# The state scans of a two-layer mixer run three heads ahead of attention instead of one

## The reference

```python
def s5_branch(u, ...):                      # state branch, 512 channels, 2048 complex states
    lam_bar = jnp.exp(lam * dt)
    bu = jnp.einsum('gph,bsgh->bsgp', b_bar, ug)
    _, h = lax.associative_scan(combine, (a, bu), axis=1)       # h[t] = lam_bar*h[t-1] + bu[t]
    y = jnp.real(jnp.einsum('ghp,bsgp->bsgh', c_mat, h)) ...
    y = jax.nn.gelu(y + d * uf)
    return y * jax.nn.sigmoid(y @ glu_w + glu_b)

def hybrid_mixer(x, ...):
    proj = x @ w_in                          # gives z_sgu, z_ssm, q, k, v, gates
    br_a = spatial_gating(jax.nn.gelu(z_sgu), ...)
    br_b = s5_branch(z_ssm, ...)
    br_c = moba_attention(q, k, v)           # 8 heads of 64, here plain causal attention
    g = sigmoid(gates)
    merged = g[0] * (br_a @ w_a) + g[1] * (br_b @ w_b) + g[2] * (br_c @ w_c)
    return merged @ w_out
```

## Time and profile before

| what | value |
|---|---|
| median of 3 runs | 2191.64 us (2191.57 to 2194.16) |
| profiled execution | 2188.97 us, span 2187.2 us |
| busy over the span | PE 94%, DVE 39%, ACT 21%, POOL 11% |
| mean granted TensorE clock | 0.974 of full speed |

### The profile page before, as it was taken

The page is one execution under the profiler, slowest core; times in us unless marked ns, Lnnn a source line. Parts: engine busy times, 40 slices in busy tenths (PEclk is TensorE's granted clock), DMA queues, the critical chain, the costliest instruction groups (busy, mean ns, idle before and its releaser), DMA issues.

```text
span 2187.2 us, 34182 instructions
## 1 busy us (share of the span) xinstructions
PE 2061.2 (94%) x13823; PEld 1387.8 (63%) x13823; DVE 847.5 (39%) x1551; ACT 469.6 (21%) x880; POOL 248.0 (11%) x233
## 2 busy tenths in 40 slices
PE   7988999999998999999889999999997999999996
PEld 5776868864676786886344565699985443444342
DVE  1288230001237822000238865645456333233324
ACT  2255200000325510000032125433333101110110
POOL 2367100000037700000000001100000000000000
PEclk9999999999999999999989999999997899999998
DMA  7422444442642254444452224400012899999993
GB/s 236 149 83 89 179 138 154 154 154 85 199 145 91 83 192 140 150 149 149 153 188 74 92 100 154 155 3 4 3 44 87 336 396 395 395 412 395 392 395 154
DMA packets 138672, 385.45 MB, mean 176 GB/s; under 512 B 16903, under 2 KB 64367, under 8 KB 127409
## 3 DMA queue, kind: packets, MB, share of 16 engines
q1 hardware_dynamic: 138545, 383.61, 47.2%
HBM read 382.54 MB, written 1.05 MB: 175 GB/s over the span
## 4 chain that ended last, share of the span: by engine, by line
PE 41%; DVE 5%; ACT 2%; issue 1%; DMA 1%; DVEq 0%; POOL 0%; ACTq 0%; POOLq 0%
PE psum L1243 9%; PE psum L2820 9%; PE psum L1990 8%; PE psum L2844 5%; PE psum L2755 3%; PE psum L1442 1%; PE psum L2406 1%; ACT arena L1600 1%; PE psum L2059 1%; DVE arena L3033 1%; DVE arena L2955 1%; PE psum L2832 1%; PE psum L2008 1%; DMA ring<-in_w_ada_dram 1%; PE psum L2773 0%
## 5 line engine op out<-in xcount | busy, mean ns | idle before, releaser
L364 PE MATMUL psum<-arena,ring 128*128 128x256 f32 x1728 | 389.4, 385 | 17.2 <-DVE arena L935 15.9
L364 PEld LDWEIGHTS psum<-arena,ring 128*128 128x128 f32 x1728 | 330.3, 192 | 73.5 <-issue 16.6
L573 PE MATMUL psum<-arena,ring 128*128 128x256 f32 (+1 forms) x1536 | 306.8, 361 | 3.2 <-ACT arena L624 3.2
L573 PEld LDWEIGHTS psum<-arena,ring 128*128 128x128 f32 x1536 | 270.5, 189 | 39.3 <-ACT arena L624 4.0
L1990 PE MATMUL psum<-arena 64*64 64x64 f32 (+1 forms) x4320 | 179.9, 237 | 4.6 <-issue 1.9
L624 ACT ACTIVATE arena<-psum 128x512 f32<-128x512 f32 (+2 forms) x116 | 62.9, 567 | 542.2 <-PE psum L573 264.0
L1990 PEld LDWEIGHTS psum<-arena 64*64 64x64 f32 x4320 | 171.6, 134 | 6.8 <-issue 3.1
L600 PE MATMUL psum<-ring,arena 128*128 128x512 f32 x352 | 151.4, 592 | 0.0
L1243 PE MATMUL psum<-arena,ring 128*128 128x512 f32 (+2 forms) x432 | 142.2, 489 | 0.0
L1013 DVE TENSOR_TENSOR arena<-arena,psum 128x512 f32<-128x512 f32 x22 | 15.2, 690 | 288.8 <-PE psum L573 288.8
L600 PEld LDWEIGHTS psum<-ring,arena 128*128 128x128 f32 x352 | 66.9, 190 | 83.3 <-issue 83.2
(11 more groups left out here) (416 smaller groups left out, 2573.3 us busy)
## 6 DMA issues: line engine op xcount, KB each, us to landing
ring<-in_w_in_dram SPq DMA_DIRECT2D x31, 2048.0 KB, 8.1
ring<-in_ffn_w_dram SPq DMA_DIRECT2D x46, 1024.0 KB, 6.5
arena<-in_ex_gate_dram SPq DMA_DIRECT2D x15, 2048.0 KB, 11.2
arena<-in_ex_up_dram SPq DMA_DIRECT2D x15, 2048.0 KB, 15.7
arena<-in_ex_down_dram SPq DMA_DIRECT2D x15, 2048.0 KB, 17.5
ring<-in_ex_gate_dram SPq DMA_DIRECT2D x14, 2048.0 KB, 10.5
ring<-in_ex_up_dram SPq DMA_DIRECT2D x14, 2048.0 KB, 15.0
ring<-in_ex_down_dram SPq DMA_DIRECT2D x14, 2048.0 KB, 7.7
```

What stands on the lines that cost most here:

```text
L364: ins = pe.matmul(bank[:, j, :], w[:, kc, c * P:(c + 1) * P], moving[:, kc, :], start=kc == 0, stop=kc == k - 1)
L573: ins = pe.matmul(bank[:, j, tokens], both[:, i * DC + kc, j * P:(j + 1) * P], K.xT[:, kc, tokens], start=kc == 0, stop=kc == DC - 1)
```

## The change

1. A constant `AHEAD = 3`. PE issues `state_inputs` 0, 1 and 2 between the halves of the projections of q and k, and `state_inputs(n + 3)` in head n. DVE runs scans 0 to 2 ahead of the mix products, and `scan(n + 3)` in head n. ACT runs rotations 0 to 2 among the drains of u, of the input matrices and of q, and `rotation(n + 3)` in head n, now right behind the exponentials and ahead of the gates. POOL computes `angles(n + 3)` in head n.
2. Third buffers for cosine, sine and the two state tiles, a second one for the angle: `rotation(n)` waits for `turn_back(n - 3)`, `angles(n)` for `rotation(n - 2)`.
3. `state_outputs` comes in even heads, behind `attend_out`. DVE drains y still in odd heads, but between the scan and the division.
4. The drained signal of the first bank of a scan is given with that of the second.

The arithmetic of every instruction stays as it is.

```diff
-    keys += [("q", i) for i in range(2)]
-    keys += [None] * (len(keys) % BANKS == BANKS - 1) + [("bu", 0, c) for c in range(2)]
-    keys += [("k", i) for i in range(2)] + [("av", i) for i in range(2)]
+    for n, key in enumerate((("q", 0), ("q", 1), ("k", 0))):
+        keys += [key]
+        keys += states(n)
+    keys += [("k", 1)] + [("av", i) for i in range(2)]
...
-        if n < 7:
-            keys += [None] * (len(keys) % BANKS == BANKS - 1) + [("bu", n + 1, c) for c in range(2)]
+        if n < HEADS - AHEAD:
+            keys += states(n + AHEAD)
...
-        if n % 2 == 1:
+        if n % 2 == 0:
+            keys += [("o", n // 2 - 1)] if n > 0 else []
             keys += [("y", n // 2)]
-        elif n > 0:
-            keys += [("o", n // 2 - 1)]
...
+            act.wait_ge(K.sem["angle"], K.count("angle", l, n + 1))
+            if n >= 3:
+                act.wait_ge(K.sem["h_ready"], K.count("h_ready", l, n - 2))
...
         for i in range(2):
+            rotation(i)
             drain(("u", i), K.uT[:, 2 * i:2 * i + 2, :], ACT.Gelu_apprx_tanh, src=pairs)
...
+        rotation(2)
         for i in range(2):
             drain(("q", i), K.qT[:, 2 * i:2 * i + 2, :], src=pairs)
...
                                     accum_out=K.rowsum[:, n % 2, 1:2]).then_inc(K.sem["exped"], 1)
+            if n < HEADS - AHEAD:
+                rotation(n + AHEAD)
             for g in GATES_WITH[n]:
...
-            if n:
-                pool.wait_ge(K.sem["cos_sin"], K.count("cos_sin", l, n))
+            if n >= 2:
+                pool.wait_ge(K.sem["cos_sin"], K.count("cos_sin", l, n - 1))
...
-        angles(0)
-        angles(1)
+        for n in range(AHEAD):
+            angles(n)
...
-            if n < 6:
-                angles(n + 2)
+            if n < HEADS - AHEAD:
+                angles(n + AHEAD)
             turn_back(n)
...
-            for i in range(2):
-                dve.wait_ge(K.empty(("bu", n, i)), K.drained_count(("bu", n, i), l))
+            dve.wait_ge(K.empty(("bu", n, 1)), K.drained_count(("bu", n, 1), l))
+            dve.sem_inc(K.empty(("bu", n, 0)), 1)
...
-            if n < 7:
-                scan(n + 1)
+            if n < HEADS - AHEAD:
+                scan(n + AHEAD)
+            if n % 2 == 1:
+
+                c = n // 2
+                dve.wait_ge(K.full(("y", c)), K.full_count(("y", c), l))
...
-    K.cos, K.sin, K.g_re, K.g_im = (tile(2, BANK) for _ in range(4))
-    K.h_re, K.h_im = tile(2, BANK), tile(2, BANK)
+    K.cos, K.sin = tile(3, BANK), tile(3, BANK)
+    K.g_re, K.g_im = tile(2, BANK), tile(2, BANK)
+    K.h_re, K.h_im = tile(3, BANK), tile(3, BANK)
...
-    K.angle, K.pool_tmp = tile(BANK), tile(2, BANK)
+    K.angle, K.pool_tmp = tile(2, BANK), tile(2, BANK)
```

More of the change, by code:

```diff
@@ L377, in tokens, with project @@
                 ins.then_inc(K.full((name, tt)), 1)
-        def project(name, unit):
+        def project(name, unit, halves=range(2)):
             pe.wait_ge(K.landed(("w_in", unit)), K.landed_count(("w_in", unit), l))
             w = K.weights(("w_in", unit), DC, BANK)
-            for i in range(2):
+            for i in halves:
                 channels((name,), i, w, K.xT)
@@ L449, in state_outputs @@
                         ins = pe.matmul(bank[jj * 32:jj * 32 + 32, 0:T], w[:, b, jj * 32:jj * 32 + 32],
-                                        h[:, half, j * T:(j + 1) * T], start=i == 0, stop=i == 1)
+                                        h[:, (2 * b + half) % 3, j * T:(j + 1) * T], start=i == 0, stop=i == 1)
             ins.then_inc(K.full(("y", b)), 1)
         state_inputs(0)
-        project("k", 4)
+        project("q", 3, [1])
+        state_inputs(1)
+        project("k", 4, [0])
+        state_inputs(2)
+        project("k", 4, [1])
         tokens("av", 5)
@@ L519, in layer_tensor @@
                 attend_scores(n)
-            if n < 7:
-                state_inputs(n + 1)
+            if n < HEADS - AHEAD:
+                state_inputs(n + AHEAD)
             for g in GATES_WITH[n]:
@@ L525, in layer_tensor @@
                 attend_values(n - 1)
-            if n % 2 == 1:
+            if n % 2 == 0:
+                if n > 0:
+                    attend_out(n // 2 - 1)
                 state_outputs(n // 2)
-            elif n > 0:
-                attend_out(n // 2 - 1)
         def branch(x, name):
@@ L647, in layer_scalar, with rotation @@
         act.activation(K.sv[:, 6, :], K.sv[:, 4, :], ACT.Sin, scale=TWO_PI).then_inc(K.sem["ssm_trig"], 1)
+        def rotation(n):
+            act.wait_ge(K.sem["angle"], K.count("angle", l, n + 1))
+            if n >= 3:
+                act.wait_ge(K.sem["h_ready"], K.count("h_ready", l, n - 2))
+            angle = K.angle[:, n % 2, :]
+            act.activation(K.sin[:, n % 3, :], angle, ACT.Sin, scale=TWO_PI)
+            act.activation(angle, angle, ACT.Abs).then_inc(K.link_act.sem, 1)
+            act.wait_ge(K.link_act.sem, K.link_act.count())
+            act.activation(K.cos[:, n % 3, :], angle, ACT.Sin, scale=-TWO_PI, bias=K.half_pi).then_inc(K.sem["cos_sin"], 1)
+        K.link_act = Chain(K.act_done, 0, l, ACT_LINKS)
         for i in range(2):
+            rotation(i)
             drain(("u", i), K.uT[:, 2 * i:2 * i + 2, :], ACT.Gelu_apprx_tanh, src=pairs)
@@ L911, in scan @@
             ins.then_inc(K.sem["scanned"], 1)
-        scan(0)
         dve.wait_ge(K.sem["v_std"], K.count("v_std", l))
@@ L920, in layer_vector @@
         ins.then_inc(K.sem["v_norm"], 1)
+        for n in range(AHEAD):
+            scan(n)
         for i in range(2):
```

51 lines of the change are left out of this document (20 added, 31 removed).

## The result

| | before | after |
|---|---|---|
| median of 5 runs each, on one chip | 2191.57 us | 2205.6 us (2203.7 to 2206.27) |
| ratio | | 1.0064, 95% interval 1.0052 to 1.0075 |
| span of the profiled execution | 2187.2 us | 2203.8 us |
| mean granted TensorE clock | 0.974 | 0.969 |

The change makes the kernel slower, by 14.0 us; the forecast was 14.4. Lines moved a little: `state_inputs` is L437 now, gates and projections L369, `state_outputs` L454, the first scores L494, `w_out` L571; on DVE the scores are L947 to L954, the scan L904 to L922, the drain of y L961, the division L964 to L967; the transposes of the input matrices are L421.

A forecast was written before the change was run, and what follows sets the result against it. PE, busy 94% of the span, was taken as the bound. New waits of 1.4 + 9 + 7.8 us replace 11.1, so w_out starts 7.2 us later a layer; 14.4 on the median 2191.64 gives 2206.0 us, range 2195 to 2218.

The forecast's parts named there:

- The old ring: POOL and ACT: rotation waits for turn_back, the next angles for rotation, 17.5 us a turn; third buffers take it apart.
- The new ring: DVE-ACT-DVE, once a head: maxima, exponentials, table load, rotation, scan, division; turns of 18.8, 19.3 and 20.1 us.
- PE at the banks: PE waits for banks that DVE frees: some 9 us at state_inputs(5), 7 to 8 at state_inputs(6), 1.4 before.
- The mis-sized term: PE's transposes after DVE's input-matrix multiplications, with POOL's angles 1 and 2 now beside these: 0 to 0.9 us a layer.
- the sum: w_out starts 7.2 us later in a layer, 14.4 in two; put on the median 2191.64, this gives 2206.0 us.
- The break-even turn: DVE's turn of 17.0 us, each scan 2.4 us shorter, leaves the time unchanged; below it is faster, chance 0.11.
- The meetings of POOL with L942: Rival: POOL's last product meets DVE's scaled maxima, 1.06 us in two or three turns a layer; 2214 us, chance 0.11.
- The load that holds for more than its row: Rival: a table load keeps ACT twice its row in the heads' turns, 5.2 us a layer; 2216 us, chance 0.02.
- The three more table loads ahead of the heads: On ACT, 3.9 us lying beside PE's projections, so put at no cost; uncovered they would cost 3.9 us.

The follow-up runs named there:

- the buffers alone: Kernel before with only the third cosine, sine and state buffers, second angle tile and their waits, every order kept: 2158.8 us, ratio 0.9853.
- narrow products: Changed kernel with most of POOL's turning back of states 2, 3 and 4 cut to 32 of 512 columns: 2187.8 us, ratio 0.9981.
- rotation first: Changed kernel with ACT's rotation(n + 3) moved ahead of its wait for head n's maxima: 2176.9 us, ratio 0.9928.
- Angles late: Changed kernel with POOL waiting for the input matrices ahead of angles(1) and angles(2): 2199.1 us, ratio 1.0031.

## Why the prediction was right, and which terms were off

**The old ring opens: right.** No `state_outputs` waits for POOL any more, ACT's rotation waits for nothing in heads 0 to 2, and the buffers alone gave 33 us. My text took the gain of an open ring as what the new one would leave of it, and never worked it out by itself.

**The new ring: right in each term.** Turns of 18.8, 18.8 and 20.2 us were forecast as 18.8, 19.3 and 20.1. The waits for the rotation were 4.45, 4.27 and 5.62 us (4.4, 4.4 and 5.7 forecast), the scans 11.45, 11.57 and 11.62 (11.4). The extra 0.5 in the second turn was not there: the drain of y took it, but a scaling (L966) of 1.05 us in the first turn took 0.67 in the second. Three turns: 57.8 for 58.2. That the 11.4 come from POOL is shown by the narrow products, that the ring as a whole sets the time by rotation first.

**PE at the banks: right.** `state_inputs(5)` waited 8.96 (9), `(6)` 7.37 (7 to 8), the gate ahead of them 2.05 (1.4). From `state_inputs(6)` to `w_out` it was 293.91 - 171.33 = 122.6 us (122.8).

**The mis-sized term: the transposes of the input matrices.** I gave them 0 to 0.9 us a layer and put 0 into the sum, on the ground that one product of POOL would lie under the multiplications. Five of DVE's instructions met POOL's angles 1 and 2, and the wait was 2.3 us a layer. In the second layer the clock fell behind it: the eight transposes and the 32 matmuls after them took 1.97 and 7.82 us, for 1.09 and 7.10 in the first layer, 1.6 us more. So the term is 4.6 us of waits and 1.6 of clock in the two layers. I had the row of the multiplications' last instruction, and did not lay POOL's three instructions of an angle beside all that DVE does there.

Angles late took these 6.2 us away and put 2.0 back at the first `state_inputs`. In the profiled executions its second `w_out` starts 8.0 us earlier than the changed kernel's: 4.2 are this difference, 1.6 the fall of the clock at 661 us (below), which it did not have, and the rest is not traced.

**Why the sum still came out: by luck.** In the first layer `w_out` starts at 293.91, 9.3 us later than in the earlier trace rows, not 7.2: the first scores come 4.8 us later instead of 2.1, and from there the way is 4.5 us longer instead of 5.1. Up to the second `w_out` another 13.1 are lost. The second layer of the changed kernel:

```profile
610.20 1.97 PE L421 MATMUL psum<-arena 128*128 128x128 f32 x8 [2.31 <-DVE arena L875]
611.97 7.82 PE L369 MATMUL psum<-arena,ring 128*128 128x256 f32 x32
...
661.22 2.08 PE L479 MATMUL psum<-arena 128*128 128x128 f32 x8
...
845.88 14.43 PE L571 MATMUL psum<-ring,arena 128*128 128x512 f32 x33 [1.51 <-DVE arena L981]
```

and the kernel before:

```profile
823.44 27.73 PE L562 MATMUL psum<-ring,arena 128*128 128x512 f32 x64 [1.51 <-DVE arena L969]
```

The difference between the layers is mostly clock: 1.6 us behind the transposes' wait, and 1.6 at the matmuls from 661 us on, ahead of which PE had not stood. Together that makes 22.4 us at the second `w_out`, where the prediction had 14.4. But the whole span grew by 16.6 only: 3.9 us come back between there and the second block's products, where PE, after waits that both kernels have, does the same matmuls at different clocks (before, 32 of them in 6.30 us, after, in 3.69), and 2.0 later. On the medians it is 14.0. So the forecast of 14.4 fits the medians better than its own steps do: what the sum left out met a part behind the layers that ended a few microseconds earlier, for which nothing in the change is known to be the reason, and a median of the kernel before that lies 2.6 us above its profiled execution.

**The break-even turn.** I put it at 17.0 us. With narrow products the mean turn was 15.4, and `w_out` started 283.08 against 284.59 us before: only 1.5 earlier. The transposes' 2.3 us and the later first scores are what was missing; with them it is near 16.

**The rivals.** The meetings of POOL with L942 did not occur in the ring: L954 took 0.17 us in heads 0 to 3 (in head 5 of the first layer, behind the ring, it took 1.23). The load that holds for more than its row did not occur either. The three more table loads ahead of the heads cost nothing: PE stands nowhere between the transposes at 61.38 us and the wait ahead of the gate at 132.31.

## What to carry to other kernels

Before moving work ahead, look for what closes the ring: a second buffer of one small tile, with every order kept, brought 22 us, while the deeper order cost 47 against its own buffers. When an instruction is moved behind a hand-over (maxima to ACT, exponentials back), add up the round trip through the other engine, and ask whether the moved work needs that hand-over at all; rotation n + 3 did not. And when a bank wait is cured and the time stays, the bank was only where the wait stood.

## What the runs showed of the hardware that was not expected

- The granted clock also fell where PE had not stood still. In the second layer of the changed kernel three stretches from 625 to 655 us read 1.00 with PE busy all the while, and the next, just as busy, reads 0.83. The fall lies in its last 4 us: from 661 to 665 us the clock is 0.57, close to the 1.2 GHz level, and the eight matmuls of L479 take 2.08 us there and 1.16 at 659.08. The next stretch, 665 to 670 us, reads 1.00 again. What set it is not known:

```profile
655.00:665.00 10.00, 10.00 (x38) 0.83 0.57 194
```

- Behind waits of one length the clock is not always the same. The 32 matmuls of a gate behind the wait of 2.05 us for head 1's scores took 7.20 us in the first layer of the changed kernel and 8.88 in the second.
- A short instruction of DVE that meets POOL can take many times its own length. The 16-column product L850, 0.18 us alone in the kernel before, took 0.90 us: it started 0.20 us behind a 512-column TENSOR_TENSOR of POOL (52.32 to 53.39 us) and ended 0.03 us after it. So the price of a meeting is not a share of DVE's own instruction; here it is what POOL's still had to run.
- A TENSOR_SCALAR of POOL, which takes 1.92 us alone, took 2.13 beside DVE's multiplications, and the one of DVE's that it met 0.98 instead of 0.69. Beside a TENSOR_TENSOR of POOL it is 1.80. So not each of POOL's instructions costs DVE the same.
